# One broadcast matmul in place of two: the cached-key scores of a decoder trunk

## The chip, the cores and the metric

The kernel runs on 1 core of one Trainium2 chip. The metric is device time in microseconds (us) of one launch, taken as the median of several runs. Five engines work beside each other and meet at semaphores: TensorE (PE, matmuls), VectorE (DVE), ScalarE (ACT), GpSimd (POOL) and SyncE (SP), which issues most of the DMAs here; POOL issues the rest. Each engine works strictly in its own order.

## The reference

A two-layer decoder trunk in fp32 for 512 prompt tokens and 32 sample tokens (8 sequences of 4), width 1024. Layer 0 mixes by pooling; layer 1 is dilated attention with three head groups. Cut to the part that the change touches, the keys and values are projected once, and the sample queries see 128 cached keys of each group beside the new ones:

```python
kv_new = (x @ attn_w_kv).reshape(b, n, N_DIL_GROUPS, 2, HEADS_PER_GROUP, HEAD_DIM)
for g in range(N_DIL_GROUPS):
    kv_g = jnp.concatenate([kv_past[g], kv_new[:, :, g]], axis=1)
    kv_groups.append((kv_g[:, :, 0], kv_g[:, :, 1]))
...
idx = rows[:, None] - steps[None, :]
kg = jnp.take(k, idx, axis=1, mode='clip')
s = jnp.einsum('bqhd,bqkhd->bhqk', q_blk, kg)
```

In group 0 (dilation 1) all four queries of a sequence look at the same cached keys. In groups 1 and 2 (dilation 4 and 16) each of the four looks at keys of its own.

## The kernel before, in words

**Products.** Every linear layer is computed from split operands: a value is a high part (rounded to fp32r) and a low part (what is left). `products` (L602) runs, for each of 8 chunks k of 128 input features, three pairs of matmuls (high weight by high input, high by low, low by high), each pair covering the 544 tokens as 2 x 272 columns. Such a step is called an eighth here, and `products` of one 128-wide output chunk a unit. Weights arrive by DMA in `raw[s]`, s = 0 or 1; ACT writes the high part (`round_hi`, L1060), DVE the low part (`round_lo`, L1342), and SP may load `raw[s]` anew once the low part is made (`stream`, L464).

**The key/value stage** has 12 turns i, each of two units, s = 0 and s = 1. On PE (`kv_turn`, L833) a turn is: unit 0 of turn i, the transposes of chunk s = 1 of turn i-1, unit 1, the transposes of chunk s = 0. `kv_transposes` (L789) turns a feature-major chunk `kvt[s]` to token-major: four 128 x 128 transposes for the prompt (L794) and one piece for the 32 samples (L796). That piece is an ordinary fp32 matmul by the identity, which writes 32 partitions of a bank of `pc`, partitions 0 to 31 for s = 0 and 32 to 63 for s = 1. A transpose is told to the hardware as such by `nc.tensor.transpose`; the plain `matmul` at L796 is not. ACT evacuates both (`kv_tokens`, L1241), and SP stores them.

**Scores on cached keys** ride in turns 2 to 9, one sequence b in each (b = 0 to 7). Group 0: PE turns the sequence's 128 keys (`turn_keys`, L802), DVE copies them (L1564), PE multiplies (`key_scores`, L810). Groups 1 and 2: for each of 8 steps t (2 groups x 4 queries) the query's row must stand on all 128 partitions beside the keys. `cast_queries` (L820) does that on PE. The stationary operand is a one-hot tile `sel[s]` of 32 rows x 128 columns that picks one of 32 query rows, and the moving operand is the 32 query rows, 512 columns. Since the rows are split in a high and a low part (`q_hi`, `q_lo`, 32 rows each), it takes two matmuls of 512 columns into one bank (L829). Then DVE multiplies with the keys (L1544, `times`) and sums (L1552, `summed`). Steps 1 to 4 ride in unit 0, one in front of every second eighth, and steps 5 to 8 in unit 1. The order written out for DVE (`kv_turn`, L1555) puts the two weight roundings of a turn between those: the low part for s = 1 behind `times` of step 2, and for s = 0 of the next turn behind `times` of step 6:

```python
                if t == 2:
                    round_lo("kv", 1, i)
                if t == 6:
                    round_lo(nxt, 0, j)
                summed(b, t)
```

PE may overwrite the bank for step t + 1 only when `times` of step t is done (`kq_made`, L827). On ACT (`kv_turn`, L1251) a turn is: evacuate unit 0, `round_hi` for s = 0 of the next turn, tokens of s = 1, evacuate unit 1, `round_hi` for s = 1, tokens of s = 0. On SP (L535) the weights of turn i + 1 for s = 0 stand behind the store of the tokens of s = 0 of turn i - 1.

**Loading keys.** POOL, when sequence b is done, writes the one-hot tile and the group-0 queries for sequence b + 2 (`queries`, L1769) and then issues its keys' load, three DMAs of 2.25 MB together (`load`, L1757). For sequences 0 and 1 this stands ahead of the stage, so the loads for sequences 2 to 7 are issued at the start of turns 3 to 8 of the stage.

Of the kernel before, what the change touches and what calls it, by code (L numbers as in the profile page):

```python
# [42 lines left out]
GW = HEADS * DH  # L43
# [113 lines left out]
def build(nc, A, O):  # L157
# [3 lines left out]
    def sb(where, name, shape, dt=F32):  # L161
        return where.enter_context(nc.sbuf_tensor("t_" + name, shape, dt))

    def sem(name):
        return ctx.enter_context(nc.semaphore(name))

    with ctx:
# [8 lines left out]
        ident = sb(ctx, "ident", [P, P])  # L176
# [4 lines left out]


        rq = ExitStack()
        q_hi = sb(rq, "q_rows_hi", [SAMP, 2 * GW], F32R)
        sel = [sb(rq, "one_hot0", [SAMP, DEC_S, P], F32R)]
        rq.close()
        elem = sb(ctx, "elementwise", [P, 3 * T])
        sg, hf, sq = (elem[:, j * T:(j + 1) * T] for j in range(3))
        tab = sb(ctx, "bias_rows", [HEADS, NG, RP])
        s_bias = sb(ctx, "samp_bias", [P, NG * (P + BW)])  # L190
        s_sc = sb(rq, "samp_scores", [P, NG, 256])
        q_lo = sb(rq, "q_rows_lo", [SAMP, 2 * GW], F32R)
        sel += [sb(rq, "one_hot1", [SAMP, DEC_S, P], F32R)]
        rq.close()
        work = sb(ctx, "work", [P, 5 * T])
        accs, accq, mean, var, rstd = (work[:, j * T:(j + 1) * T] for j in range(5))
# [48 lines left out]
        kvt = [sb(hq, f"kv_feat{s}", [P, T]) for s in range(2)]  # L245
# [27 lines left out]
        kv_n = sb(rx, "kv_new", [SAMP, NG * 2 * GW])  # L273
# [15 lines left out]
        pa, pb, pc, pd = ps  # L289
# [60 lines left out]
        kv_t = [sem(f"kv_transposed{s}") for s in range(2)]  # L350
        kv_tok = [sem(f"kv_tok_ready{s}") for s in range(2)]
# [22 lines left out]
        kc_ok = sem("cached_keys_evacuated")  # L374
        kc_used = sem("cached_keys_used")
        qrow_t = sem("q_rows_turned")
        qhi_ok = sem("q_rows_hi")
        qlo_ok = sem("q_rows_lo")
        q_cast = sem("q_on_all_partitions")
# [221 lines left out]
        def _(pe):  # L601
# [131 lines left out]
            for g, out in enumerate((pa[:, 0, :], pa[:, 1, :], pb[:, 0, :])):  # L733
                m = nc.tensor.matmul(out[0:HEADS, 0:RP], rbx[:, g * HEADS:(g + 1) * HEADS], oh_t[:, g, :],
                                     start=True, stop=True)
            m.then_inc(tab_mm, 1)
            for v in range(6):
                for half, cols in enumerate((slice(0, NG * P), slice(NG * P, NG * (P + BW)))):
                    m = nc.tensor.matmul(pc[:, half, 0:cols.stop - cols.start], rb_s[:, v, :], oh_s[:, v, cols],
                                         start=v == 0, stop=v == 5)  # L740
# [12 lines left out]
            for c in range(DC):  # L753
                m = nc.tensor.transpose(pc[0:PAD + SAMP, c // 4, (c % 4) * P:(c % 4 + 1) * P], utail[:, c, :], ident[:])
            m.then_inc(utail_t, 1)

            for g in range(4):
                for s in range(2):
# [5 lines left out]
                    m = products(ps[s], s, 2, lambda k: phi[:, 2 * g + k, :], lambda k: plo[:, 2 * g + k, :], at=2 * g)  # L764
# [24 lines left out]
            def kv_transposes(s, i, first=False):  # L789
                pe.wait_ge(kv_evac[s], i + 1)  # L790
                if not first:
                    pe.wait_ge(kv_tok[s], 2 * i)
                for j in range(QB):
                    nc.tensor.transpose(ps[2 + s][:, 0, j * P:(j + 1) * P], kvt[s][:, j * P:(j + 1) * P], ident[:])  # L794

                nc.tensor.matmul(pc[SAMP * s:SAMP * (s + 1), 1, 0:P], kvt[s][:, SEQ:T], ident[:], start=True,  # L796
                                 stop=True).then_inc(kv_t[s], 1)

# [19 lines left out]
            def cast_queries(b, s, t):  # L820

                g, i = (t - 1) // 4, (t - 1) % 4
                if t == 1:
                    pe.wait_ge(qb_ok, b + 1)
                    pe.wait_ge(kc_ok, b + 1)
                else:
                    pe.wait_ge(kq_made, (NCK - 1) * b + t - 1)  # L827
                for n, part in enumerate((q_hi, q_lo)):
                    m = nc.tensor.matmul(pd[:, 1, :], sel[s][:, i, :], part[:, g * GW:(g + 1) * GW], start=n == 0,  # L829
                                         stop=n == 1)  # L830
                m.then_inc(q_cast, 1)

            def kv_turn(i, b=None, s=0):  # L833

# [19 lines left out]
            for g in range(2):  # L854
                for c in range(GC):
                    m = nc.tensor.transpose(pc[0:SAMP, g, c * P:(c + 1) * P], qt[:, (g + 1) * GC + c, SEQ:T], ident[:])
# [2 lines left out]
            kv_units(0, 0, True)  # L859
            kv_units(1, 0, True)  # L860
            pe.wait_ge(qlo_ok, 1)
            kv_transposes(0, 0, True)
            kv_units(0, 1)
            kv_transposes(1, 0, True)
# [40 lines left out]
            for g in range(NG):  # L905
                for c in range(GC):
                    row = pb[0:SAMP, g // 2, (g % 2) * 256:(g % 2 + 1) * 256]
                    m = nc.tensor.matmul(row.rearrange("p (b c n) -> p b c n", b=DEC_B, c=GC)[:, :, c, :],
                                         kn_t[:, g * GC + c, :],
                                         q_bd[:, g * GC + c, :].rearrange("p (b n) -> p b n", b=DEC_B),  # L910
                                         start=True, stop=True)
# [33 lines left out]
            for c in range(GC):  # L945
                for g in range(NG):
# [3 lines left out]
                                         start=g == 0, stop=g == NG - 1)  # L950
# [106 lines left out]
        def _(act):  # L1057
# [127 lines left out]
            for c in range(DC):  # L1185
                s = c % 2
# [54 lines left out]
            def kv_tokens(s, i, first=False):  # L1241
                act.wait_ge(kv_t[s], i + 1)
                if not first:
                    act.wait_ge(kv_out[s], 32 * i)
                nc.scalar.activation(kvp[s][:].rearrange("p j n -> p (j n)"), ps[2 + s][:, 0, :], ACT.Copy) \
                    .then_inc(kv_tok[s], 1)
                nc.scalar.activation(kv_n[:, bass.ds((2 * i + s) * P, P)], pc[SAMP * s:SAMP * (s + 1), 1, 0:P],
                                     ACT.Copy) \
                    .then_inc(kv_tok[s], 1)

            def kv_turn(i, stored, nxt, j, keys=None, b=None):  # L1251
# [4 lines left out]
                kv_tokens(0, i)  # L1256

            act.wait_ge(qrow_t, 1)
            nc.scalar.activation(q_hi[:], pc[0:SAMP].rearrange("p a n -> p (a n)"), ACT.Copy).then_inc(qhi_ok, 1)
            kv_chunk(0, 0, 0, "kv", 1, True, keys=0)  # L1260
            kv_chunk(1, 0, 0, "kv", 1, True, keys=0)
            kv_tokens(0, 0, True)
# [76 lines left out]
        def _(dve):  # L1339
# [190 lines left out]
            def q_turn(i, nxt, j):  # L1530
# [4 lines left out]


            dve.wait_ge(qhi_ok, 1)
            nc.vector.tensor_tensor(q_lo[:], pc[0:SAMP].rearrange("p a n -> p (a n)"), q_hi[:].bitcast(F32), ALU.subtract) \
                .then_inc(qlo_ok, 1)

            def times(b, s, t):

# [168 lines left out]
        def _(pool):  # L1711
# [51 lines left out]
            def load_keys(b, s):  # L1763
                load(b, cached[s][:, 0, :], cached[s][:, 1:NCK, :], 0, cached_in[s])
# [2 lines left out]
                load(b, v_c0[s][:], v_c[s], 1, value_in[s])  # L1767

            def queries(b, s):  # L1769
                nc.gpsimd.tensor_copy(sel[s][:], ident[0:SAMP, bass.ds(DEC_S * b, DEC_S)].unsqueeze(2)  # L1770
                                      .to_broadcast([SAMP, DEC_S, P]))
                nc.gpsimd.tensor_copy(q_b[s][:], q_bd[:, 0:GC, bass.ds(2 * DEC_S * b, 2 * DEC_S)]).then_inc(qb_ok, 1)

            for s in range(2):
                pool.wait_ge(w_used[s], FIRST["kv"])
            load_keys(0, 0)
            load_keys(1, 1)
            nc.gpsimd.memset(q_bd[:], 0.0).then_inc(qbd_ok, 1)
            pool.wait_ge(qbd_ok, 1)
            pool.wait_ge(q_evac, NG * GC)  # L1780
# [71 lines left out]
```

## Time and profile before

| | us |
|---|---|
| median of 3 runs | 2517.81 |
| lowest, highest run | 2512.13, 2519.68 |
| span of the profiled execution | 2516.9 |
| PE busy in it | 2315.5 (92%) |
| DVE, ACT, POOL busy | 920.3, 680.1, 262.3 |
| DMA over the span | 99 GB/s |

The profiled execution has no time of its own beside its span; the span is 0.9 us under the median and within the runs' spread, so it is taken for its time. In the rows below, `128*32` behind an operation is rows by columns of the part of the PE array that it uses, and `128x512` partitions by elements. The start of a record is when the engine took it up; matmuls are pipelined, so the distance from one start to the next, and not the duration, is what one costs in a stream. The printed code carries the line numbers of the profile.

### The profile page before, as it was taken

Reading aid. Unit: us, or ns where it says so; the run is one execution under the profiler, and the core shown is the slowest. Engines: PE = TensorE matmul, PEld = TensorE weight load, DVE = VectorE, ACT = ScalarE, POOL = GpSimd, SP = SyncE. Lnnn points to the kernel's source line nnn. Section 1 sums busy time; section 2 is a strip of 40 time slices with the busy share of each in tenths; the row PEclk is TensorE's granted clock in tenths of the full one; section 3 lists DMA queues with packets and bytes.
Section 4 is the critical chain, followed back from the end, with each engine's and each line's share of the span. In section 5 each row is a group of like instructions: output and inputs, shape, how many; then the busy total and the mean of one; then the engine's idle time right before and its main releaser. Section 6 shows DMA issues by size and latency. Waiting matters only on the chain.

```text
span 2516.9 us, 42260 instructions
## 1 busy us (share of the span) xinstructions
PE 2315.5 (92%) x17471; PEld 2168.3 (86%) x17471; DVE 920.3 (37%) x1176; ACT 680.1 (27%) x956; POOL 262.3 (10%) x241
## 2 busy tenths in 40 slices
PE   7559999978799999979999989999988988999997
PEld 5559999978799999979999979877854468999996
DVE  2113332276633332243333233366433344333324
ACT  3112222233422222232222223222222234222212
POOL 0000001211300001210000230111011040000022
PEclk9779999989899999989999999999979998999998
DMA  3542233212222233232323342565464222232331
GB/s 98 80 92 83 87 97 92 75 59 62 62 87 85 84 100 90 77 127 87 88 87 93 91 134 71 180 196 180 146 213 140 90 67 59 83 92 83 98 92 47
DMA packets 376249, 248.81 MB, mean 99 GB/s; under 512 B 7807, under 2 KB 360423, under 8 KB 375631
## 3 DMA queue, kind: packets, MB, share of 16 engines
q1 hardware_dynamic: 366087, 209.95, 29.3%
q0 software_dynamic: 10096, 37.94, 4.3%
q8 instruction: 47, 0.77, 0.1%
q14 instruction: 19, 0.15, 0.0%
HBM read 225.91 MB, written 22.31 MB: 99 GB/s over the span
## 4 chain that ended last, share of the span: by engine, by line
PE 85%; DMA 6%; DVE 5%; ACT 2%; issue 1%; SPq 1%; POOL 1%; DVEq 0%; POOLq 0%; ACTq 0%
PE pair L610 71%; DMA t_w_raw<-in_ffn_w 4%; PE pair L630 3%; PE pair L962 3%; PE pair L829 2%; DVE t_stream L1434 1%; PE pair L709 1%; PE pair L887 1%; DMA t_w_raw<-in_attn_w_kv 1%; DVE t_work L1436 1%; PE pair L985 1%; PE pair L995 1%; ACT t_w_hi L1068 1%; DVE t_w_lo L1348 1%; DMA t_bias<-scratch_bias_rows 1%
## 5 line engine op out<-in xcount | busy, mean ns | idle before, releaser
L1348 DVE TENSOR_TENSOR t_w_lo<-t_w_raw,t_w_hi 128x1024 fp32r<-128x1024 f32 (+2 forms) x302 | 421.3, 1395 | 834.8 <-ACT t_w_hi L1068 834.7
L610 PE MATMUL pair<-t_x_hi,t_w_hi 128*128 128x272 f32 x2944 | 618.5, 292 | 66.0 <-DVE t_w_lo L1348 63.5
L610 PE MATMUL pair<-t_x_lo,t_w_hi 128*128 128x272 f32 x2944 | 613.1, 289 | 0.0
L610 PE MATMUL pair<-t_x_hi,t_w_lo 128*128 128x272 f32 x2944 | 612.6, 289 | 0.0
L1068 ACT ACTIVATE t_w_hi<-t_w_raw 128x1024 fp32r<-128x1024 f32 (+2 forms) x302 | 336.3, 1114 | 947.1 <-PE pair L610 842.4
L610 PEld LDWEIGHTS pair<-t_x_hi,t_w_hi 128*128 128x128 f32 x2944 | 466.1, 190 | 67.9 <-DVE t_w_lo L1348 57.3
L610 PEld LDWEIGHTS pair<-t_x_lo,t_w_hi 128*128 128x128 f32 x2944 | 470.6, 191 | 0.0
L610 PEld LDWEIGHTS pair<-t_x_hi,t_w_lo 128*128 128x128 f32 x2944 | 465.5, 190 | 0.0
L610 PE MATMUL pair<-t_h_hi,t_w_hi 128*128 128x272 f32 x1408 | 292.2, 289 | 0.0
L610 PE MATMUL pair<-t_h_lo,t_w_hi 128*128 128x272 f32 x1408 | 290.3, 287 | 0.0
L610 PE MATMUL pair<-t_h_hi,t_w_lo 128*128 128x272 f32 x1408 | 290.0, 287 | 0.0
L1723 POOL TENSOR_TENSOR t_work<-t_work,t_stream 128x544 f32<-128x544 f32 x42 | 59.1, 1408 | 1613.9 <-DVE t_stream L1410 1612.4
L610 PEld LDWEIGHTS pair<-t_h_lo,t_w_hi 128*128 128x128 f32 x1408 | 222.1, 188 | 0.0
L610 PEld LDWEIGHTS pair<-t_h_hi,t_w_hi 128*128 128x128 f32 x1408 | 219.7, 188 | 0.0
L610 PEld LDWEIGHTS pair<-t_h_hi,t_w_lo 128*128 128x128 f32 x1408 | 219.7, 188 | 0.0
L1107 ACT ACTIVATE t_elementwise<-pair 128x544 f32<-128x544 f32 x88 | 55.0, 625 | 387.5 <-PE pair L610 387.5
L1399 DVE TENSOR_TENSOR t_elementwise<-t_elementwise,pair 128x544 f32<-128x544 f32 x88 | 63.4, 721 | 261.7 <-PE pair L610 260.9
L1410 DVE SCALAR_TENSOR_TENSOR t_stream<-pair,t_stream 128x544 f32 (+1 forms) x48 | 34.8, 725 | 218.0 <-PE pair L610 218.0
L630 PE MATMUL pair<-t_x_hi,t_w_hi 128*128 128x272 f32 x192 | 45.0, 319 | 63.1 <-DVE t_x_lo L1449 63.1
L1725 POOL TENSOR_TENSOR t_work<-t_work,t_elementwise 128x544 f32<-128x544 f32 x42 | 102.7, 2444 | 0.0
L630 PEld LDWEIGHTS pair<-t_x_hi,t_w_hi 128*128 128x128 f32 x192 | 34.4, 215 | 65.3 <-issue 65.3
L610 PE MATMUL pair<-t_kv_in_hi,t_w_hi 128*128 128x272 f32 x384 | 89.2, 313 | 0.0
(222 smaller groups left out, 2223.9 us busy)
## 6 DMA issues: line engine op xcount, KB each, us to landing
t_w_raw<-in_ffn_w SPq DMA_DIRECT2D x176, 512.0 KB, 3.8
t_w_raw<-in_ffn_w SPq DMA_DIRECT2D x64, 704.0 KB, 4.5
t_cached<-in_cache_kv_w POOLq DMA_DIRECT2D x16, 1024.0 KB, 9.3
t_cached_v<-in_cache_kv_w POOLq DMA_DIRECT2D x16, 1024.0 KB, 8.1
t_w_raw<-in_attn_w_kv SPq DMA_DIRECT2D x24, 512.0 KB, 6.9
t_w_raw<-in_attn_w_q SPq DMA_DIRECT2D x12, 512.0 KB, 3.7
scratch_bias_rows<-t_bias_rows SPq DMA_DIRECT2D x3, 1536.0 KB
t_w_raw<-in_pool_w_in SPq DMA_DIRECT2D x8, 512.0 KB, 3.6
```

The lines of the kernel that those rows point to most:

```text
L610: m = nc.tensor.matmul(out[:, j, 0:HALF], w[:, at + k, :], a(k)[:, j * HALF:(j + 1) * HALF], start=first and k == 0 and n == 0, stop=last ...
L630: m = nc.tensor.matmul(ps[s][:, j, 0:HALF], w[:, k, :], a[:, k, j * HALF:(j + 1) * HALF], start=k == 0 and n == 0, stop=k == DC - 1 and n ...
L709: m = nc.tensor.matmul(out[:, j, 0:HALF], invd[:], a[:, j * HALF:(j + 1) * HALF], start=first, stop=not first)
L829: m = nc.tensor.matmul(pd[:, 1, :], sel[s][:, i, :], part[:, g * GW:(g + 1) * GW], start=n == 0, stop=n == 1)
L962: m = nc.tensor.matmul(pd[32 * s:32 * s + 32, 0, :], p_b[s][:, t, :], v_c0[s][:] if t == 0 else v_c[s][:, t - 1, :], start=t == 0, stop=t ...
L1068: nc.scalar.activation(whi[s][:, 0:KT[stage], :], raw[s][:, 0:KT[stage], :], ACT.Copy) \
L1107: nc.scalar.activation(split(sg[:]), halves(pa), ACT.Silu).then_inc(gate_silu, 1)
L1348: nc.vector.tensor_tensor(wlo[s][:, 0:k, :], raw[s][:, 0:k, :], whi[s][:, 0:k, :].bitcast(F32), ALU.subtract).then_inc(lo_made[s], 1)
L1399: nc.vector.tensor_tensor(split(hf[:]), split(sg[:]), halves(pb), ALU.mult).then_inc(h_made, 1)
L1410: nc.vector.scalar_tensor_tensor(out=split(x[:, c, :]), in0=halves(out), scalar=scale, in1=split(x[:, c, :]), op0=ALU.mult, op1=ALU.add) \
L1723: nc.gpsimd.tensor_tensor(accs[:], accs[:], x[:, c, :], ALU.add).then_inc(acc_made, 1)
L1725: nc.gpsimd.tensor_tensor(accq[:], accq[:], sq[:], ALU.add).then_inc(acc_made, 1)
```

## The change

The high and low query rows are stacked in one tile `q_hl` of 128 partitions: rows 0 to 31 high, 32 to 63 low, 64 to 127 zero. The one-hot tiles become 128 x 4 x 128, with the one-hot twice (rows 0 to 31 and 32 to 63) and zero below, so that one matmul over all 128 rows adds high and low part. The one-hots are now cut from `id2`, the 32 x 32 identity twice. POOL builds `id2` and the zeros once, ahead of its q-block work, and PE waits for that (`qsel_ok`) before its first transposes of the stage. The samples' piece of `kv_transposes` becomes a real transpose, always to partitions 0 to 31, with s = 0 in columns 0 to 127 and s = 1 in columns 128 to 255 of the same bank; PE now also waits, ahead of the transposes of one s, until ACT has evacuated the tokens of the other s before it.

```diff
-        q_hi = sb(rq, "q_rows_hi", [SAMP, 2 * GW], F32R)
-        sel = [sb(rq, "one_hot0", [SAMP, DEC_S, P], F32R)]
+        q_hl = sb(rq, "q_rows", [P, 2 * GW], F32R)
+        sel = [sb(rq, "one_hot0", [P, DEC_S, P], F32R)]
...
-        q_lo = sb(rq, "q_rows_lo", [SAMP, 2 * GW], F32R)
-        sel += [sb(rq, "one_hot1", [SAMP, DEC_S, P], F32R)]
+        sel += [sb(rq, "one_hot1", [P, DEC_S, P], F32R)]
+        id2 = sb(rq, "ident_twice", [2 * SAMP, SAMP])
...
                 if not first:
                     pe.wait_ge(kv_tok[s], 2 * i)
+                if not (first and s == 0):
+                    pe.wait_ge(kv_tok[1 - s], 2 * (i + s))
...
-                nc.tensor.matmul(pc[SAMP * s:SAMP * (s + 1), 1, 0:P], kvt[s][:, SEQ:T], ident[:], start=True,
-                                 stop=True).then_inc(kv_t[s], 1)
+                nc.tensor.transpose(pc[0:SAMP, 1, s * P:(s + 1) * P], kvt[s][:, SEQ:T], ident[:]).then_inc(kv_t[s], 1)
...
-                for n, part in enumerate((q_hi, q_lo)):
-                    m = nc.tensor.matmul(pd[:, 1, :], sel[s][:, i, :], part[:, g * GW:(g + 1) * GW], start=n == 0,
-                                         stop=n == 1)
-                m.then_inc(q_cast, 1)
+                nc.tensor.matmul(pd[:, 1, :], sel[s][:, i, :], q_hl[:, g * GW:(g + 1) * GW], start=True, stop=True) \
+                    .then_inc(q_cast, 1)
...
             pe.wait_ge(qlo_ok, 1)
+            pe.wait_ge(qsel_ok, 3)
             kv_transposes(0, 0, True)
...
-                nc.gpsimd.tensor_copy(sel[s][:], ident[0:SAMP, bass.ds(DEC_S * b, DEC_S)].unsqueeze(2)
-                                      .to_broadcast([SAMP, DEC_S, P]))
+                nc.gpsimd.tensor_copy(sel[s][0:2 * SAMP], id2[:, bass.ds(DEC_S * b, DEC_S)].unsqueeze(2)
+                                      .to_broadcast([2 * SAMP, DEC_S, P]))
...
+            for h in range(2):
+                part = slice(SAMP * h, SAMP * h + SAMP)
+                nc.gpsimd.tensor_copy(id2[part], ident[part, part]).then_inc(qsel_ok, 1)
+            nc.gpsimd.memset(q_hl[2 * SAMP:P, :].bitcast(F32), 0.0)
+            for s in range(2):
+                m = nc.gpsimd.memset(sel[s][2 * SAMP:P].bitcast(F32), 0.0)
+            m.then_inc(qsel_ok, 1)
+            pool.wait_ge(qsel_ok, 3)
```

The ACT copy of the high rows, the DVE subtraction for the low rows and the ACT evacuation of the samples' piece only change the places that they read and write.

PE, the first broadcast of turn 2 and the group-0 scores behind it, before:

```order
L610 MATMUL pair<-t_kv_in_hi,t_w_lo 128x272 x2
L829 MATMUL pair<-t_q_rows_hi,t_one_hot 128x512 [waits cached_keys_evacuated,q_blocks_b_ready]
L829 MATMUL pair<-t_q_rows_lo,t_one_hot 128x512
L610 MATMUL pair<-t_kv_in_hi,t_w_hi 128x272 x2
L610 MATMUL pair<-t_kv_in_lo,t_w_hi 128x272 x2
L610 MATMUL pair<-t_kv_in_hi,t_w_lo 128x272 x2
L815 MATMUL pair<-t_q_blocks_b,t_k_turned 128x8 [waits cached_keys_evacuated,q_blocks_b_ready]
```

The same place now (lines of the changed kernel stand one or two lower):

```order
L611 MATMUL pair<-t_kv_in_hi,t_w_lo 128x272 x2
L830 MATMUL pair<-t_q_rows,t_one_hot 128x512 [waits cached_keys_evacuated,q_blocks_b_ready]
L611 MATMUL pair<-t_kv_in_hi,t_w_hi 128x272 x2
L611 MATMUL pair<-t_kv_in_lo,t_w_hi 128x272 x2
L611 MATMUL pair<-t_kv_in_hi,t_w_lo 128x272 x2
L817 MATMUL pair<-t_q_blocks_b,t_k_turned 128x8 [waits cached_keys_evacuated,q_blocks_b_ready]
```

One matmul is gone at each of the 64 places like this one, and nothing else moved between them.

POOL, behind the issue of the first keys and ahead of the first one-hots, as a piece of the difference:

```order
 L1761 DMA t_cached<-in_cache_kv_w 128x4x512
-L1778 MEMSET t_q_blocks 128x768
-L1783 COPY t_q_blocks<-t_q_feat 64x384 [waits q_evac,q_blocks_ready]
-L1783 COPY t_q_blocks<-t_q_feat 64x384
-L1770 CAST t_one_hot<-t_ident 32x512 [waits q_blocks_ready]
+L1780 COPY t_ident_twice<-t_ident 32x32 x2
+L1781 MEMSET t_q_rows 64x1024
+L1783 MEMSET t_one_hot 64x512 x2
+L1786 MEMSET t_q_blocks 128x768 [waits one_hots_zeroed]
+L1791 COPY t_q_blocks<-t_q_feat 64x384 [waits q_evac,q_blocks_ready]
+L1791 COPY t_q_blocks<-t_q_feat 64x384
+L1770 CAST t_one_hot<-t_ident_twice 64x512 [waits q_blocks_ready]
```

Five small operations come in front of the q-block work, and the one-hot copies cover 64 partitions in place of 32.

## Rows read from the trace of the kernel before

**Rows 1.** The page: busy time by engine, and the chain that ended last, by line.

```profile
PE 2315.5 (92%) x17471; PEld 2168.3 (86%) x17471; DVE 920.3 (37%) x1176; ACT 680.1 (27%) x956; POOL 262.3 (10%) x241
...
PE pair L610 71%; DMA t_w_raw<-in_ffn_w 4%; PE pair L630 3%; PE pair L962 3%; PE pair L829 2%; DVE t_stream L1434 1%; PE pair L709 1%; PE pair L887 1%; DMA t_w_raw<-in_attn_w_kv 1%; DVE t_work L1436 1%; PE pair L985 1%; PE pair L995 1%; ACT t_w_hi L1068 1%; DVE t_w_lo L1348 1%; DMA t_bias<-scratch_bias_rows 1%
```

**Rows 2.** Windows: start:end, us; busy (x count) by engine; PEclk, DMA share, GB/s.

```profile
1660.00:1680.00 20.00, 19.87 (x125) 15.48 (x124) 11.46 (x18) 4.83 (x10) 2.81 (x5) 1.00 0.64 208
```

**Rows 3.** Timeline of PE, a broadcast and the eighths around it: start us, us, what.

```profile
1647.74 0.42 PE L610 MATMUL pair<-t_kv_in_hi,t_w_lo 128*128 128x272 f32 x2
1648.08 0.50 PE L829 MATMUL pair<-t_q_rows_hi,t_one_hot 32*128 32x512 f32 x1
1648.42 0.39 PE L829 MATMUL pair<-t_q_rows_lo,t_one_hot 32*128 32x512 f32 x1
1648.74 0.52 PE L610 MATMUL pair<-t_kv_in_hi,t_w_hi 128*128 128x272 f32 x2
1649.09 0.41 PE L610 MATMUL pair<-t_kv_in_lo,t_w_hi 128*128 128x272 f32 x2
...
1650.10 0.42 PE L610 MATMUL pair<-t_kv_in_hi,t_w_lo 128*128 128x272 f32 x2
1650.44 0.50 PE L829 MATMUL pair<-t_q_rows_hi,t_one_hot 32*128 32x512 f32 x1
```

**Rows 4.** Timeline of PE: start of one turn and of the next.

```profile
1662.36 0.60 PE L794 MATMUL pair<-t_ident,t_kv_feat 128*128 128x128 f32 x4
1662.89 0.41 PE L796 MATMUL pair<-t_ident,t_kv_feat 128*32 128x128 f32 x2
1663.22 0.66 PE L807 MATMUL pair<-t_ident,t_cached 128*128 128x128 f32 x4
...
1684.66 0.60 PE L794 MATMUL pair<-t_ident,t_kv_feat 128*128 128x128 f32 x4
```

**Rows 5.** Timeline of PE: turning the sample queries ahead of the stage.

```profile
1590.07 1.05 PE L856 MATMUL pair<-t_ident,t_q_feat 128*32 128x128 f32 x8 [0.71 <-ACT t_q_feat L1224]
1590.88 0.50 PE L610 MATMUL pair<-t_kv_in_hi,t_w_hi 128*128 128x272 f32 x2
```

**Rows 6.** Timeline of ACT in the turn that starts at 1662.36.

```profile
1674.92 0.62 ACT L1238 ACTIVATE t_kv_feat<-pair 128x544 f32<-128x544 f32 x1
1676.71 1.06 ACT L1068 ACTIVATE t_w_hi<-t_w_raw 128x1024 fp32r<-128x1024 f32 x1 [1.17 <-DMA t_w_raw<-in_attn_w_kv]
```

**Rows 7.** Timeline of the SP queue in that turn.

```profile
1665.73 0.93 SPq L468 DMA_DIRECT2D t_w_raw<-in_attn_w_kv  x1
```

**Rows 8.** Waits, 1625 to 1830 us: total us, times, longest us.

```profile
ACT t_w_hi L1068 <- DMA t_w_raw<-in_attn_w_kv: 5.9, 6, 1.6
```

**Rows 9.** Windows of 2 us in that turn, as in rows 2.

```profile
1670.00:1672.00 2.00, 2.00 (x14) 1.47 (x12) 1.85 (x4) 0.00 (x0) 0.00 (x0) 1.00 0.98 376
```

**Rows 10.** Timeline of DVE in that turn.

```profile
1679.18 0.69 DVE L1544 TENSOR_TENSOR t_k_times_q<-pair,t_cached 128x512 f32<-128x512 f32 x1 [0.85 <-PE pair L829]
1679.79 1.22 DVE L1348 TENSOR_TENSOR t_w_lo<-t_w_raw,t_w_hi 128x1024 fp32r<-128x1024 f32 x1
...
1681.55 0.69 DVE L1544 TENSOR_TENSOR t_k_times_q<-pair,t_cached 128x512 f32<-128x512 f32 x1
```

**Rows 11.** Timeline of POOL ahead of the first turn.

```profile
1594.07 0.79 POOL L1778 MEMSET t_q_blocks<- 128x768 f32 x1
...
1596.11 0.60 POOL L1770 CAST t_one_hot<-t_ident 32x512 fp32r<-32x512 f32 x1
```

**Rows 12.** Timeline of PE: the first turn with broadcasts starts.

```profile
1618.64 0.66 PE L807 MATMUL pair<-t_ident,t_cached 128*128 128x128 f32 x4 [0.67 <-DVE t_w_lo L1348]
```

**Rows 13.** Timeline of ACT behind the stage.

```profile
1829.99 0.60 ACT L1245 ACTIVATE t_kv_tok<-pair 128x512 f32<-128x512 f32 x1 [4.16 <-DMA out_kv_p<-t_kv_tok]
```

**Rows 14.** Windows of the attention behind the stage, as in rows 2.

```profile
1880.00:1900.00 20.00, 17.89 (x138) 9.29 (x138) 6.33 (x19) 3.79 (x7) 5.29 (x16) 1.00 0.58 172
1900.00:1920.00 20.00, 19.15 (x120) 9.00 (x123) 8.04 (x26) 5.65 (x13) 0.00 (x0) 0.83 0.33 112
```

More of the change, by code:

```diff
@@ L376, in build @@
         qrow_t = sem("q_rows_turned")
+        qsel_ok = sem("one_hots_zeroed")
         qhi_ok = sem("q_rows_hi")
@@ L1246, in kv_tokens @@
                     .then_inc(kv_tok[s], 1)
-                nc.scalar.activation(kv_n[:, bass.ds((2 * i + s) * P, P)], pc[SAMP * s:SAMP * (s + 1), 1, 0:P],
-                                     ACT.Copy) \
+                nc.scalar.activation(kv_n[:, bass.ds((2 * i + s) * P, P)], pc[0:SAMP, 1, s * P:(s + 1) * P], ACT.Copy) \
                     .then_inc(kv_tok[s], 1)
@@ L1258, in _ @@
             act.wait_ge(qrow_t, 1)
-            nc.scalar.activation(q_hi[:], pc[0:SAMP].rearrange("p a n -> p (a n)"), ACT.Copy).then_inc(qhi_ok, 1)
+            nc.scalar.activation(q_hl[0:SAMP, :], pc[0:SAMP].rearrange("p a n -> p (a n)"), ACT.Copy).then_inc(qhi_ok, 1)
             kv_chunk(0, 0, 0, "kv", 1, True, keys=0)
@@ L1537, in _ @@
             dve.wait_ge(qhi_ok, 1)
-            nc.vector.tensor_tensor(q_lo[:], pc[0:SAMP].rearrange("p a n -> p (a n)"), q_hi[:].bitcast(F32), ALU.subtract) \
-                .then_inc(qlo_ok, 1)
+            nc.vector.tensor_tensor(q_hl[SAMP:2 * SAMP, :], pc[0:SAMP].rearrange("p a n -> p (a n)"),
+                                    q_hl[0:SAMP, :].bitcast(F32), ALU.subtract).then_inc(qlo_ok, 1)
             def times(b, s, t):
```

## The prediction

> **What bounds the kernel now.** I read the page first. PE is busy 92% of the span, and the chain that ended last lies on PE for most of its length; the broadcasts, L829, are 2% of it, some 50 us [rows 1]. Then the windows of the key/value stage, because the change lives there alone. From 1660 to 1680 us PE is busy 19.87 of 20 us at the full granted clock, the DMA engines 0.64 and DVE 11.46 of 20 us [rows 2]. So in this stage PE is the bound, and time taken off PE comes off the end, until another engine is late. Then the timeline of a turn on PE for the prices, and last ACT, SP and DVE in the same turn, to see who is late next.
>
> **What a broadcast costs.** From one broadcast to the next is 1648.08 to 1650.44, 2.36 us. In it lie two eighths, six pairs of matmuls. Four pairs take 1649.09 to 1650.10, 1.01 us, so a pair takes 0.2525 us and six take 1.515 us. The broadcast costs the rest, **0.845 us**, although its two matmuls start only 0.34 us apart [rows 3]. The remainder sits at the edges: 0.34 us from the last pair to the broadcast, and 0.35 us for the first pair behind it, where 0.25 is usual. The new one has all 128 rows and the same fp32r type as its neighbours. Its matmul is the kind of L610: 272 columns start 0.126 us apart, of which 0.113 are the columns at 2.4 GHz, so 512 columns take 0.213 + 0.013 = 0.227 us; I take 0.24. The upper bound: only one of the two starts goes and the edges stay, 0.845 - 0.34 = 0.505 us. Between them I take the low end, since the row it is nearest to is a full-array fp32r matmul in a stream. The saving is 0.6 us a broadcast (0.34 to 0.62), 4.8 us in a turn of eight.
>
> The Trainium skill (TensorE: Matmul & The Clock Gate, Part 3, The mechanism) has a rule against this: a weight load overlaps a running matmul only if its row group differs. Its Part 2 (LDWEIGHTS) prices a load at columns over 1.2 GHz, an estimate of 107 ns for 128. With full-array operands every broadcast would carry that load in the open, 0.33 us, and the sum would be 2 us smaller (16 broadcasts and the six last ones below, 0.09 each). The trace disagrees: L610 changes 128-column weights before every matmul and still starts one each 0.126 us [rows 3].
>
> **The samples' transposes.** Today the four prompt transposes and the sample piece take 0.53 + 0.33 = 0.86 us [rows 4]. L856, eight real transposes of the 128*32 shape that the new ones have, takes 0.81 us, 0.10 each [rows 5]. At that pace the four are 0.41, so 0.12 of the 0.53 is an edge ahead of the other kind of matmul. The new group is 0.41 + 0.10, plus 0.05 for what edge is left: 0.56 us, **0.3 us** less (bounds: 0, if a lone one costs what L796 does, and 0.34).
>
> The Trainium skill (TensorEngine Tiling (Array Packing), Restrictions) excludes the transpose mode for fp32 when columns are tiled. By it the piece would stay as dear as it is and some 2.7 us of the sum would go. Eight such f32 pieces at 0.10 us speak against it [rows 5].
>
> **A turn if PE alone decides.** A turn lasts 1662.36 to 1684.66, 22.30 us [rows 4]. It loses 4.8 and 2 x 0.3: 16.9 us.
>
> **Who is late next.** In the turn from 1662.36 ACT evacuates unit 0 at 1674.92 and then waits 1.17 us for the weights of s = 0; it starts rounding at 1676.71, 14.35 us after the turn began [rows 6]. Six turns have that wait, 0.98 us on average [rows 8], so the mean is 14.2. They are the six in which POOL loads keys. SP issued these weights at 1665.73, 3.4 us into the turn [rows 7], tied to the tokens of the turn before and not to the broadcasts, and they share the DMA engines with 2.25 MB of keys, which run at 0.98 busy and 376 GB/s [rows 9]. Nothing here gets faster by the change: the weights still land 14.2 us into the turn. Behind that stands a chain that is covered now: rounding on ACT 1.06 us; the low part on DVE, then `summed` of step 6 and `times` of step 7, which ends 1681.55 + 0.69 - 1679.79 = 2.45 us after the low part starts [rows 6, 10]; the broadcast of step 8, which PE may not start before `times` of step 7 is done, 0.05 + 0.24; the last eighth, 0.76. In sum 14.2 + 1.06 + 2.45 + 0.29 + 0.76 = **18.8 us**. PE alone wants 16.9, so PE stands idle about 1.9 us ahead of the last broadcast of these turns. They shrink by 22.3 - 18.8 = 3.5 us, six times: **21 us**. The cost of a broadcast no longer matters much in them.
>
> The other two turns with broadcasts (b = 0, whose keys came early, and b = 7, behind which no keys are loaded) have no such wait and go to 16.9: 2 x 5.4 = **10.8 us**. DVE holds there, though barely: from `times` of step 6 to the end of `times` of step 7, with the rounding between, is 1681.55 + 0.69 - 1679.18 = 3.06 us [rows 10], and PE takes two eighths and one broadcast, 1.75 + 1.5 = 3.27 us, over the same steps.
>
> The transposes outside those eight turns: the first turns end in front of L807, where PE waits 0.67 us for a weight rounding [rows 12], so nothing is won there; five groups behind the last broadcast give 5 x 0.3 = **1.5 us**.
>
> **What it adds.** POOL: three memsets of 1024, 512 and 512 elements and two small copies. A memset of 768 takes 0.79 us [rows 11], so they take 2.1 us, the copies at most 0.4. POOL's first one-hot then comes at 1598.6 in place of 1596.1, and the first broadcast is behind 1618.64 [rows 12]: nothing. PE's wait on the zeros stands behind both units of turn 0, 16 eighths from 1590.88 [rows 5], at 1603, later too. If that cover were gone it would cost the 2.5 us once. The larger one-hot copy: 32 x 512 took 0.60 us [rows 11], and cost goes by elements in a partition, so I price 64 x 512 the same; 0.6 us more in front of each key load would be the upper bound, 3.6 us. The new waits on the other s: in a turn ACT has the tokens of s = 0 done before SP's issue at 3.4 us, long before PE needs them; those of s = 1 follow the late rounding, two copies behind 15.3, at about 16 us of 18.8. In the first turns they fall where PE waits already [rows 12]. At the very end PE stands until ACT has made the last tokens of s = 0, two copies or some 0.9 us, and ACT behind it waits 4.16 us for a store anyway [rows 13]. All of it: 0.
>
> **The sum.** 21 + 10.8 + 1.5 = 33.3 us. The profiled execution had a span of 2516.9, 0.9 under the median, so from the median 2517.8 - 33.3 = **2484.5**. What follows the stage starts from the end of its last units and moves with it.
>
> **The rivals.**
> (a) The weights are not late: with PE ahead of DVE's rounding the queue meets less traffic, or they land 2 us earlier. Then all eight turns go to 16.9, 8 x 5.4 + 1.5 = 44.7: 2473. Against it: the wait stands in six of six turns with keys. Chance 0.15.
> (b) They land later, by 1 to 3 us: the other weights and the stores are issued sooner in the shorter turn and compete with the keys, and DVE has only 0.2 us of margin. Each us costs 6 us; or a broadcast stays at its upper bound, turns 19.0: 26.4 + 1.5 gives 2490. Together 2490 to 2502. Chance 0.21.
> (c) The change hardly pays: the weights land 3.5 us later in the six turns, which takes their 21 us back, and DVE's margin turns out negative in the other two. That leaves 0 to 7 us, 2510 to 2518. For it the weights would have to take 14.5 us from issue to landing in place of 11, with the same bytes beside them. Chance 0.04.
> (d) Slower: the clock. PE now stands idle 1.9 us in each of six turns. If the grant fell to 1.2 GHz from that, each such turn would pay its 16 eighths again, 16 x 0.76 = 12.1 us; three turns of six eat the whole gain, six give 2484.5 + 73 = 2557. For it: in the attention a window with PE busy 19.15 of 20 us shows 0.83. Against it: one with 17.89 shows 1.00 [rows 14], and a turn would still be 90% busy with full-array products. Chance 0.06.
> The Trainium skill (TensorE: Matmul & The Clock Gate, Part 4) says that transpose mode does not count as busy for the clock, which would add to (d) with 24 more transposes. Turns with eight of them and more run at 1.00 [rows 2].
>
> **How the numbers follow.** The forecast, 2479 to 2490, has 0.54, (a) 0.15, (b) 0.21, (c) 0.04, (d) 0.06. The range takes in (a) with 2 us for the spread of runs, and (b) up to 2502: 2471 to 2502. What a measurement can tell from no change is about 0.3%, 7.5 us. Faster by more: 0.54 + 0.15 + 0.21 = 0.90. Within: 0.04. Slower: 0.06.
>
> **What would show it.** Right: broadcasts followed by a pair after 0.24 us; sample transposes 0.10 us; turns of 18.8 us where keys are loaded and 16.9 where not; DVE's low part for s = 0 waiting about 2 us for ACT, ACT for the weights about 3 us, and PE for `times` ahead of the last broadcast; DMA share about 0.75 over a turn. Wrong: even turns of 16.9 us (a); ACT's wait above 4 us (b); a granted clock under 1.00 between 1620 and 1790 us (d).

## The result, and the profile after

| | before | after |
|---|---|---|
| median, us | 2517.57 (4 runs) | 2487.08 (4 runs) |
| span of the profiled execution, us | 2516.9 | 2486.0 |
| PE busy, us | 2315.5 | 2271.2 |

The medians are 30.5 us apart. The ratio of the times, estimated from the single runs, is 0.9874, with a 95% interval of 0.9861 to 0.9888; the quotient of the medians, 0.9879, lies in it. So the changed kernel is faster, by 1.1 to 1.4%. (The kernel before was run once more beside it, so its median is of four runs now.) The page of the kernel after, its first lines and its chain, to be read against [rows 1]:

```profile
PE 2271.2 (91%) x17383; PEld 2157.6 (87%) x17383; DVE 917.7 (37%) x1176; ACT 679.4 (27%) x956; POOL 265.9 (11%) x246
...
PE pair L611 68%; DMA t_w_raw<-in_ffn_w 4%; PE pair L631 3%; PE pair L963 3%; DMA t_w_raw<-in_attn_w_kv 3%; DVE t_stream L1434 1%; PE pair L710 1%; PE pair L888 1%; DVE t_work L1436 1%; PE pair L986 1%; ACT t_w_hi L1069 1%; PE pair L996 1%; DVE t_u_sum L1476 1%; DMA t_bias<-scratch_bias_rows 1%; DVE t_w_lo L1348 0%
```

The broadcasts, 2% of the chain before, no longer stand among its parts; the load of the key/value weights has 3% in place of 1%. That is the story in one line: time went off PE, and a DMA came forward. PE is busy for 44 us less, and only 31 us of that reach the end. (Lines of the changed kernel stand one to three lower on PE and ACT: L611 for L610, L797 for L794, L799 for L796, L809 for L807, L830 for L829, L1069 for L1068.)

The timeline of PE after, one broadcast and the next, answers [rows 3]:

```profile
1659.64 0.42 PE L611 MATMUL pair<-t_kv_in_hi,t_w_lo 128*128 128x272 f32 x2
1659.89 0.40 PE L830 MATMUL pair<-t_q_rows,t_one_hot 128*128 128x512 f32 x1
1660.13 0.41 PE L611 MATMUL pair<-t_kv_in_hi,t_w_hi 128*128 128x272 f32 x2
...
1661.39 0.42 PE L611 MATMUL pair<-t_kv_in_hi,t_w_lo 128*128 128x272 f32 x2
1661.65 0.50 PE L830 MATMUL pair<-t_q_rows,t_one_hot 128*128 128x512 f32 x1
```

From broadcast to broadcast is 1.76 us, less six pairs of 0.2525 leaves **0.245 us** for the broadcast, where it was 0.845. The pair ahead and the pair behind are at their usual distance: 1659.64 to 1659.89, 1660.13 to 1660.38 (not shown). The edges are gone. The group of transposes in the middle of the turn, which answers [rows 4]:

```profile
1662.75 0.60 PE L797 MATMUL pair<-t_ident,t_kv_feat 128*128 128x128 f32 x4
1663.19 0.27 PE L799 MATMUL pair<-t_ident,t_kv_feat 128*32 128x128 f32 x1
1663.21 0.50 PE L611 MATMUL pair<-t_kv_in_hi,t_w_hi 128*128 128x272 f32 x2
1663.56 0.41 PE L611 MATMUL pair<-t_kv_in_lo,t_w_hi 128*128 128x272 f32 x2
```

It takes 0.46 us from its first transpose to the next product, 0.09 us for each of five. The same group in the middle of a turn took 0.87 us before. The group at the start of a turn, up to the turning of the keys (L807, now L809), went from 0.86 to 0.54 us.

The starts of turns on PE, same view. The first two rows enclose a turn with a key load (b = 5), the last two the one without (b = 7):

```profile
1711.04 0.60 PE L797 MATMUL pair<-t_ident,t_kv_feat 128*128 128x128 f32 x4
...
1729.63 0.60 PE L797 MATMUL pair<-t_ident,t_kv_feat 128*128 128x128 f32 x4
...
1747.53 0.60 PE L797 MATMUL pair<-t_ident,t_kv_feat 128*128 128x128 f32 x4
...
1764.51 0.60 PE L797 MATMUL pair<-t_ident,t_kv_feat 128*128 128x128 f32 x4
```

The eight turns last 17.1, 19.1, 20.5, 19.2, 18.0, 18.6, 17.9 and 17.0 us. The six in the middle load keys; their mean is 18.9. All eight were 22.3.

Why the six are longer is in the turn from 1653.40, in which three engines hand one delay on. ACT first, waiting for the weights:

```profile
1668.33 1.06 ACT L1069 ACTIVATE t_w_hi<-t_w_raw 128x1024 fp32r<-128x1024 f32 x1 [4.28 <-DMA t_w_raw<-in_attn_w_kv]
```

then DVE, in the order written for it:

```profile
1666.22 0.69 DVE L1544 TENSOR_TENSOR t_k_times_q<-pair,t_cached 128x512 f32<-128x512 f32 x1 [0.21 <-PE pair L830]
1669.43 1.23 DVE L1348 TENSOR_TENSOR t_w_lo<-t_w_raw,t_w_hi 128x1024 fp32r<-128x1024 f32 x1 [2.52 <-ACT t_w_hi L1069]
1670.57 0.68 DVE L1552 TENSOR_REDUCE t_samp_scores<-t_k_times_q 128x512 f32 x1
1671.16 0.68 DVE L1544 TENSOR_TENSOR t_k_times_q<-pair,t_cached 128x512 f32<-128x512 f32 x1
```

then PE, whose last broadcast of the turn needs the product at 1671.16:

```profile
1669.03 0.42 PE L611 MATMUL pair<-t_kv_in_hi,t_w_lo 128*128 128x272 f32 x2
1671.90 0.79 PE L830 MATMUL pair<-t_q_rows,t_one_hot 128*128 128x512 f32 x1 [2.46 <-DVE t_k_times_q L1544]
```

The weights land 14.9 us into this turn, the latest of the six (13.2 to 14.9, 14.1 on average; before, 13.3 to 14.6, also 14.1 on average). PE stands 2.46 us, the longest of six such gaps; the others are 0.8 to 1.93 us, and the mean is 1.5. Over the stage, the waits view of 1625 to 1790 us after, against [rows 8]:

```profile
ACT t_w_hi L1069 <- DMA t_w_raw<-in_attn_w_kv: 21.4, 7, 4.3
PE pair L830 <- DVE t_k_times_q L1544: 9.0, 6, 2.5
```

ACT's wait for weights went from 5.9 to 21.4 us, of which 20.5 us are the six turns with key loads: the weights land when they did, counted from the start of a turn, and the rest of the turn reaches them sooner.

### The profile page after: what moved, and what is told of

It is laid out like the page before. It is cut to its first block, busy times and chain, and to the rows that moved or that the text cites. A ratio compares the mean times of both kernels' runs of the same rounds, so it can differ in the third digit from the quotient of the medians.

```text
span 2486.0 us, 42096 instructions
## 1 busy us (share of the span) xinstructions
PE 2271.2 (91%) x17383; PEld 2157.6 (87%) x17383; DVE 917.7 (37%) x1176; ACT 679.4 (27%) x956; POOL 265.9 (11%) x246
## 4 chain that ended last, share of the span: by engine, by line
PE 81%; DMA 8%; DVE 5%; ACT 2%; issue 2%; SPq 1%; POOL 1%; ACTq 0%; DVEq 0%; POOLq 0%
PE pair L611 68%; DMA t_w_raw<-in_ffn_w 4%; PE pair L631 3%; PE pair L963 3%; DMA t_w_raw<-in_attn_w_kv 3%; DVE t_stream L1434 1%; PE pair L710 1%; PE pair L888 1%; DVE t_work L1436 1%; PE pair L986 1%; ACT t_w_hi L1069 1%; PE pair L996 1%; DVE t_u_sum L1476 1%; DMA t_bias<-scratch_bias_rows 1%; DVE t_w_lo L1348 0%
## 5 line engine op out<-in xcount | busy, mean ns | idle before, releaser
L611 PE MATMUL pair<-t_x_hi,t_w_hi 128*128 128x272 f32 x2944 | 616.7, 291 | 67.1 <-DVE t_w_lo L1348 64.6
L611 PE MATMUL pair<-t_x_lo,t_w_hi 128*128 128x272 f32 x2944 | 611.6, 289 | 0.0
L611 PE MATMUL pair<-t_x_hi,t_w_lo 128*128 128x272 f32 x2944 | 610.8, 289 | 0.0
L1069 ACT ACTIVATE t_w_hi<-t_w_raw 128x1024 fp32r<-128x1024 f32 (+2 forms) x302 | 336.8, 1115 | 964.3 <-PE pair L611 839.4
L611 PEld LDWEIGHTS pair<-t_x_hi,t_w_hi 128*128 128x128 f32 x2944 | 464.1, 190 | 69.0 <-DVE t_w_lo L1348 58.3
L611 PEld LDWEIGHTS pair<-t_x_lo,t_w_hi 128*128 128x128 f32 x2944 | 469.0, 190 | 0.0
L611 PEld LDWEIGHTS pair<-t_x_hi,t_w_lo 128*128 128x128 f32 x2944 | 463.9, 189 | 0.0
L611 PE MATMUL pair<-t_h_hi,t_w_hi 128*128 128x272 f32 x1408 | 292.2, 289 | 0.0
L611 PE MATMUL pair<-t_h_lo,t_w_hi 128*128 128x272 f32 x1408 | 290.3, 287 | 0.0
L611 PE MATMUL pair<-t_h_hi,t_w_lo 128*128 128x272 f32 x1408 | 290.0, 287 | 0.0
L611 PEld LDWEIGHTS pair<-t_h_lo,t_w_hi 128*128 128x128 f32 x1408 | 222.1, 188 | 0.0
L611 PEld LDWEIGHTS pair<-t_h_hi,t_w_hi 128*128 128x128 f32 x1408 | 219.7, 188 | 0.0
L611 PEld LDWEIGHTS pair<-t_h_hi,t_w_lo 128*128 128x128 f32 x1408 | 219.7, 188 | 0.0
L611 PE MATMUL pair<-t_kv_in_hi,t_w_hi 128*128 128x272 f32 x384 | 82.3, 296 | 0.0
```

Source lines behind the costliest of these rows:

```text
L611: m = nc.tensor.matmul(out[:, j, 0:HALF], w[:, at + k, :], a(k)[:, j * HALF:(j + 1) * HALF], start=first and k == 0 and n == 0, stop=last ...
L1069: nc.scalar.activation(whi[s][:, 0:KT[stage], :], raw[s][:, 0:KT[stage], :], ACT.Copy) \
```

## The experiments

Each kernel was run beside the kernel before on the same chip, whose medians there were 2516.84 us (the first four) and 2516.27 us (the last four). Theory: a broadcast's price is mostly the change of array shape, and with it gone the late weights, passed on by DVE, set the six turns. The rivals: the second matmul itself is the price; DVE's order alone sets the six turns, whatever the weights do; every microsecond of PE still counts.

**The two halves of the change apart.** The broadcast alone, with the samples' piece and the waits as before:

```diff
-                if not (first and s == 0):
-                    pe.wait_ge(kv_tok[1 - s], 2 * (i + s))
...
-                nc.tensor.transpose(pc[0:SAMP, 1, s * P:(s + 1) * P], kvt[s][:, SEQ:T], ident[:]).then_inc(kv_t[s], 1)
+                nc.tensor.matmul(pc[SAMP * s:SAMP * (s + 1), 1, 0:P], kvt[s][:, SEQ:T], ident[:], start=True,
+                                 stop=True).then_inc(kv_t[s], 1)
```

> The one-matmul broadcast alone: the samples' piece and PE's waits are those of the kernel before. Theory (in the six turns with key loads the end is set by the late weights for s = 0, through DVE, and only the turns of b = 0 and b = 7 are PE's): those two turns are 0.6 us longer than in the changed kernel (17.7 in place of 17.1 and 17.0), the six with key loads as long (mean 18.9), so the whole takes 2488 to 2489.5 us, 28 us or more under the kernel before. Rival (PE's time counts in every turn): 8 x 0.6 us, 2492 us.

Measured: 2486.86 us, ratio 0.9877 (0.9862 to 0.9893). The first turn is 17.8 us long and the six with key loads 18.75 on average, 18.3 to 19.1. So without the transposes the gain is there as far as the medians (2486.9 and 2487.1) can tell. The turns came out as expected; the total is 1 to 3 us under it. The turns at either end are 0.8 us longer than in the changed kernel, 1.6 us in all, and the medians don't show that; in the profile of the changed kernel one turn lost about as much to the clock (below), and here none did. The rival's 2492 is outside.

The transposes and the new waits alone, in the kernel before (the reverse of this diff):

> The real transposes of the samples' piece and the new waits on the other s alone; the broadcasts stay two matmuls of 32 rows. Here PE sets every turn, so both see a gain of two pieces a turn: turns of 22.3 - 2 x 0.32 = 21.7 us, eight of them 5 us, in all 2511 to 2513 us. If the new waits cost something where PE is the bound, less than that: PE would stand idle ahead of L794, which the waits view would name. Behind the stage I expect no gain, since ACT waits there for a store.

Measured: 2510.25 us, ratio 0.9974 (0.9966 to 0.9983), 6.6 us less than before. The starts of two neighbouring turns:

```profile
1680.96 0.60 PE L808 MATMUL pair<-t_ident,t_cached 128*128 128x128 f32 x4
...
1702.45 0.60 PE L808 MATMUL pair<-t_ident,t_cached 128*128 128x128 f32 x4
```

Turns of 21.5 us, 0.8 less than 22.3, so a piece saves 0.40 us and not 0.3: eight turns give 6.4 us. The same edit is worth 6.6 us where PE is the bound, and nothing in the six turns that late weights set (18.75 us without it, 18.9 with it). PE stops at the new waits twice, 1.1 us ahead of the first turn with broadcasts and 0.9 us at the very end. From the turning of the sample queries to the first turned keys it still takes 27.9 us, where it took 28.6 before, and at the end ACT waits for a store anyway, so this kernel shows no cost of them.

**What a broadcast costs.** Both matmuls kept, but padded with zeros to all rows, in the kernel before:

```diff
-        q_hi = sb(rq, "q_rows_hi", [SAMP, 2 * GW], F32R)
-        sel = [sb(rq, "one_hot0", [SAMP, DEC_S, P], F32R)]
+        q_hi = sb(rq, "q_rows_hi", [P, 2 * GW], F32R)
+        sel = [sb(rq, "one_hot0", [P, DEC_S, P], F32R)]
...
+            for rest in (slice(SAMP, 2 * SAMP), slice(2 * SAMP, P)):
+                nc.gpsimd.memset(q_hi[rest, :].bitcast(F32), 0.0)
+                nc.gpsimd.memset(q_lo[rest, :].bitcast(F32), 0.0)
+                for s in range(2):
+                    m = nc.gpsimd.memset(sel[s][rest].bitcast(F32), 0.0)
```

> The kernel before with both broadcast matmuls kept, but each over all 128 rows: one-hot, high rows and low rows are padded with zeros. Theory (most of the 0.845 us of a broadcast is at the edges, where the array changes from 128 rows to 32 and back): a broadcast costs 0.45 to 0.47 us, both matmuls start 0.23 us apart, and the first pair behind takes 0.25 us; a turn is 22.3 - 3.0 = 19.3 us, eight of them save 24 us, about 2494 us. Rival (the two matmuls cost what they do because they are two): 0.85 us stays, 2517 us.

Measured: 2493.97 us, ratio 0.9907 (0.9892 to 0.9923). PE's timeline:

```profile
1645.73 0.40 PE L830 MATMUL pair<-t_q_rows_hi,t_one_hot 128*128 128x512 f32 x1
1645.96 0.39 PE L830 MATMUL pair<-t_q_rows_lo,t_one_hot 128*128 128x512 f32 x1
1646.19 0.41 PE L611 MATMUL pair<-t_kv_in_hi,t_w_hi 128*128 128x272 f32 x2
1646.44 0.41 PE L611 MATMUL pair<-t_kv_in_lo,t_w_hi 128*128 128x272 f32 x2
```

Two matmuls in 0.46 us and no edge behind them; turns of 19.3 to 19.4 us, one of 19.9. With the same columns to stream and the same number of matmuls as before, 22.9 of the 30 us are there. So most of the gain is not the matmul saved but the rows padded. The 22.9 overstate its share, because the late weights cap what is saved further in six turns; by the price of a broadcast it is 0.38 of the 0.60 us saved.

The changed kernel with its one matmul over the 64 rows that are not zero:

```diff
-                nc.tensor.matmul(pd[:, 1, :], sel[s][:, i, :], q_hl[:, g * GW:(g + 1) * GW], start=True, stop=True) \
+                nc.tensor.matmul(pd[:, 1, :], sel[s][0:2 * SAMP, i, :], q_hl[0:2 * SAMP, g * GW:(g + 1) * GW],
+                                 start=True, stop=True) \
```

> The changed kernel, but the one broadcast matmul reads only the 64 rows that are not zero. Theory of the edges: the array changes to 64 rows and back, so a broadcast costs 0.23 + 0.1 + 0.1 + 0.1 = about 0.5 us in place of 0.24; turns of b = 0 and 7 grow by 2 us to 19.1, the six others to about 19.2 at least, in all 2491 to 2494 us. Rival (one matmul in place of two is the whole gain, the zero rows do nothing): 0.24 us, 2487 us.

Measured: 2497.04 us, ratio 0.9916 (0.9899 to 0.9933). PE's timeline:

```profile
1647.84 0.41 PE L611 MATMUL pair<-t_kv_in_hi,t_w_lo 128*128 128x272 f32 x2
1648.18 0.50 PE L830 MATMUL pair<-t_q_rows,t_one_hot 64*128 64x512 f32 x1
1648.61 0.52 PE L611 MATMUL pair<-t_kv_in_hi,t_w_hi 128*128 128x272 f32 x2
1648.97 0.42 PE L611 MATMUL pair<-t_kv_in_lo,t_w_hi 128*128 128x272 f32 x2
...
1650.33 0.50 PE L830 MATMUL pair<-t_q_rows,t_one_hot 64*128 64x512 f32 x1
```

One matmul over 64 rows costs 2.15 - 1.515 = 0.635 us, more than two over 128 rows (0.465). It has 0.09 us more than usual ahead, 0.43 from its start to the next pair where the full one has 0.24, and 0.11 more behind: 0.39 us of edges. I had put them at 0.3 or less, hence turns of 19.65 us in place of 19.1 and a total 3 us above what was expected. PE sets all eight turns here, so all are alike. Two matmuls of 32 rows pay 0.845 - 0.465 = 0.38 us over two of 128 rows, one of 64 rows pays 0.39 over one of 128: the surcharge comes once for a stay on fewer rows and not once for each matmul, which is why it is put down to the change of shape.

**Who sets the six turns.** The changed kernel with one issue on SP moved:

```diff
-                stream("kv", i)
-                if i >= 1:
-                    kt_store(i - 1, 0)
-                    if i >= 2:
-                        kv_store(i - 2, 1)
-                    kt_store(i - 1, 1)
-                    kv_store(i - 1, 0)
+                weights(i, 1)
+                kt_store(i - 1, 0)
+                if i >= 2:
+                    kv_store(i - 2, 1)
+                if i + 1 < UNITS["kv"]:
+                    weights(i + 1, 0)
+                kt_store(i - 1, 1)
+                kv_store(i - 1, 0)
```

(`weights(i, s)` is one half of `stream`; the loop runs from i = 1, with `weights(0, 0)`, `weights(0, 1)` and `weights(1, 0)` ahead of it.)

> The changed kernel with one order of SP moved: the weights for s = 0 are issued as soon as DVE has freed their buffer, near the end of the turn before, ahead of the stores of s = 1 features and s = 0 tokens and so ahead of the key load. Theory (their landing, 14.2 to 15 us into a turn, sets the six turns with key loads): ACT's wait for weights in these turns is gone, all eight turns are 17.0 us, 6 x 1.9 = 11 us less than the changed kernel, 2476 us. Rival (DVE's own order, rounding between the products of steps 6 and 7, or the DMA traffic as a whole sets them): turns of 18 us or more stay, 2483 to 2488.

Measured: **2473.16 us**, ratio 0.983 (0.9817 to 0.9844), faster than both the kernel before and the changed one. Two turn starts, and the window of 1660 to 1680 us, which answers [rows 2]:

```profile
1681.85 0.60 PE L817 MATMUL pair<-t_ident,t_cached 128*128 128x128 f32 x4
...
1698.82 0.60 PE L817 MATMUL pair<-t_ident,t_cached 128*128 128x128 f32 x4
```

```profile
1660.00:1680.00 20.00, 19.89 (x151) 19.08 (x150) 16.27 (x23) 4.66 (x11) 2.82 (x5) 1.00 0.77 256
```

All turns are 17.0 us, 17.1 at most, and PE is busy 19.89 of 20 us again, with DVE at 16.27 and the DMA engines at 0.77. From the first turned keys to the end of the eighth turn that is 11.3 us less. From the transposes of the queries ahead of the stage to the first turned keys are 26.7 us in place of 27.9, which I had left out: there the weights of turn 2 waited behind stores as well, and ACT waited 5.0 us for them, 0.3 us here. With these 1.1 us it is 12.4. (The same stretch is 28.5 and 28.6 us in the last two kernels below, whose SP order is that of the changed kernel, so it varies by 0.8 us by itself.) The medians are 43.1 and 30.5 us under those of the kernel before, 12.6 apart; the two ratios, 0.983 and 0.9874, put them 11 us apart. So the move is worth 11 to 13 us. The bytes are the same: between 1634 and 1765 us the weights take 4.0 us from issue to landing (median), and 9.1 us in the changed kernel.

The same move in the kernel before:

> The same move of SP's order in the kernel before. There PE alone sets a turn (22.3 us) and the late weights are covered, so both theories say no change: 2517.5 us, within 2 us, although ACT's wait for weights goes from 5.9 us in six turns to 0. A gain of more than 5 us would mean that the late weights cost time already before.

Measured: 2513.94 us, ratio 0.9993 (0.9984 to 1.0002). Turns of 22.3 us as before, no wait of ACT for weights left in the six turns. The interval holds 1; it reaches from 4 us less to 0.5 us more. The stretch ahead of the first turned keys is 0.7 us shorter in its profile, and nothing else of the stage is. So the move that is worth 11 to 13 us on the changed kernel is worth next to nothing here.

The changed kernel without its later key loads:

```diff
-                    load_keys(2 * n + s, s)
...
-                pe.wait_ge(cached_in[s], 24 * (b - s) + 48)
+                pe.wait_ge(cached_in[s], 48)
```

> The changed kernel without the key loads for sequences 2 to 7: their scores are computed from the keys of sequences 0 and 1, which stay in place, and 13.5 MB less are read. Theory: with no keys beside them the weights land about 4 to 5 us after their issue, 8 us into a turn, ahead of ACT's need at 10; all eight turns are 17.0 us, 2476 us, as with the moved order. Rival (DVE's order sets the six turns): they stay at 18 us or more, 2484 to 2488.

Measured: 2473.66 us, ratio 0.9827 (0.9812 to 0.9842). Two turn starts:

```profile
1684.28 0.60 PE L809 MATMUL pair<-t_ident,t_cached 128*128 128x128 f32 x4
...
1701.26 0.60 PE L809 MATMUL pair<-t_ident,t_cached 128*128 128x128 f32 x4
```

Turns of 17.0 us, and again 4.0 us from the issue of the weights to their landing. The total is 2.3 us under the 2476 expected. Taking the keys' bytes away does the same as issuing the weights ahead of them. Both leave DVE's order and work as they are, so DVE's order alone is ruled out.

DVE's rounding moved from step 6 to step 8 (`if t == 6` becomes `if t == 8`):

> The changed kernel with DVE's rounding for s = 0 of the next turn moved from behind the product of step 6 to behind that of step 8. Theory: the late weights no longer hold back the last broadcast, but unit 0 of the next turn needs the rounding at 17.5 us into the turn and the weights arrive at 14.2 to 15, high part at 16, low part at 17.5 to 18.3: six turns of 18.0 to 18.3 us in place of 18.9, 2482 to 2484 us. If the weights' landing did not matter, the move would change nothing or cost, since the copy of the turned keys then stands behind the rounding: 2487 to 2490.

Measured: 2480.93 us, ratio 0.9857 (0.9842 to 0.9873), turns of 17.7 to 18.1 us, 17.9 on average, 1 us under the changed kernel's six and 0.1 to 0.4 under what was expected; the waits view, 1625 to 1790 us:

```profile
PE pair L809 <- DVE t_w_lo L1348: 5.6, 7, 1.0
```

The last broadcast is free now, and PE waits ahead of turning the next keys (L809), 0.8 us a turn. It does not wait there for late weights, as I had expected. The first line is PE behind the turn of b = 0, whose weights came early (ACT rounds them at 1627.97); the second is DVE in a turn with a key load:

```profile
1635.85 0.66 PE L809 MATMUL pair<-t_ident,t_cached 128*128 128x128 f32 x4 [0.69 <-DVE t_w_lo L1348]
...
1688.16 1.22 DVE L1348 TENSOR_TENSOR t_w_lo<-t_w_raw,t_w_hi 128x1024 fp32r<-128x1024 f32 x1
```

PE waits 0.69 us behind the early weights as well, and DVE makes the low part without a wait for ACT in all eight turns. So here DVE's order, with the rounding as the last thing but one, sets all eight turns, at 17.7 us and more; that they came close to the 18.0 to 18.3 us forecast from the landing is luck. What the run does show is that PE's wait at the last broadcast goes when the rounding leaves its place ahead of the product of step 7. Where the consumer of a late load stands in DVE's order is worth 1 us a turn; the load in time is worth 2.

## Why the prediction was right

2484.5 us was forecast and 2487.08 measured, within the likeliest case, and the mechanism was the one forecast. Step by step:

- **The broadcast**: 0.24 us forecast, 0.245 measured. The upper bound of 0.505 fell. That full-array operands make the weight load visible, as the Trainium skill's rule on row groups has it (TensorE: Matmul & The Clock Gate, Part 3, The mechanism), is not what this case shows: 0.245 us is 512 columns and 0.03.
- **The turn where PE decides**: 16.9 forecast, 17.1 and 17.0 measured. DVE's margin of 0.2 us held.
- **The turns with key loads**: 18.8 forecast, 18.9 measured on average, and by the mechanism forecast. It is shown by two runs, weights issued earlier and keys left out, and the way through DVE by the third, its order moved. The spread, 17.9 to 20.5, was not forecast: the weights landed 13.2 to 14.9 us into a turn, and once the clock fell, which is 0.25 us of the mean. Without it the mean is 18.6, so the fit to 0.1 us is in part luck. PE's gap was put at 1.9 us and is 1.5; ACT's wait of about 3 us was 2.6 to 4.3, in one turn past the 4 us named as the sign of (b).
- **The sum over the eight turns**: 31.8 forecast, 1796.09 - 1617.04 less 1764.51 - 1617.19 = 31.7 measured.
- **The transposes**: sized at 0.3 us a piece, from the group at the start of a turn. That group did go from 0.86 to 0.54 us, but the one in the middle from 0.87 to 0.46, and a turn lost 0.8 us where PE is the bound, 0.40 a piece. In the changed kernel this hardly matters, since six of eight turns don't feel it. The rule of the Trainium skill that column tiling rules the transpose mode out for fp32 (TensorEngine Tiling (Array Packing), Restrictions) would have left this at nothing; here a group with a 128*32 transpose in it takes 0.09 us for each of its five.
- **What it adds**: nothing, as forecast. POOL's first one-hot came at 1598.44 (forecast 1598.6), and the copy over 64 partitions takes 0.61 us where the one over 32 took 0.60.
- **The step that failed** is the 1.5 us behind the last broadcast. PE's five groups there did get shorter, but what follows waits for ACT, and ACT for a store that stands in SP's queue behind eight bias loads. I had seen that wait, 4.16 us [rows 13], used it as cover for the new wait of PE, and not subtracted the gain of the same groups from it. The wait grew from 4.16 to 5.86 us. After:

```profile
1798.24 0.60 ACT L1246 ACTIVATE t_kv_tok<-pair 128x512 f32<-128x512 f32 x1 [5.86 <-DMA out_kv_p<-t_kv_tok]
```

From the end of the eighth broadcast turn to this copy are 33.9 us before and 33.7 after. The remaining 687 us to the end are 0.9 us longer after, which no run here explains; over all ten profiles of this document they are 685.7 to 690.4 us.
- **The clock rival** came true in one turn, in small. The windows of the kernel after:

```profile
1670.00:1672.00 2.00, 0.10 (x1) 0.10 (x1) 1.86 (x4) 0.03 (x1) 0.00 (x0) 0.90 0.50 146
1672.00:1674.00 2.00, 2.00 (x8) 1.90 (x9) 1.80 (x3) 0.00 (x0) 0.40 (x1) 0.50 0.06 18
```

PE stood still for 2.46 us; near the end of that the granted clock fell to 0.50, the lower of the two levels, 1.2 GHz, and stayed there until about 1675 us. Pairs took 0.45 us, and broadcast, eighth and transposes about 1.5 us more than at 1.00. In the other five turns, with gaps of up to 1.93 us, the clock stayed at 1.00. It is one event in one profile: that the gap brought it about is not tested, nor whether the other executions have it.

## What to carry to other kernels

Before counting columns of a small matmul in a dense stream, subtract: the distance between two of them less the stream between gives the true price, and here nearly half of it (0.38 of 0.845 us) was the change of array shape on either side, which zero rows to the full height remove. Once the bound engine is relieved, the size of the gain is set by the first load or rounding that was only just covered; find it by its time into the period, and ask whether its issue hangs on something it doesn't need. Here moving one issue ahead of two stores was worth nothing that the runs can tell before the change, and 11 to 13 us after it.

## What the runs showed of the hardware

A 512-column fp32r matmul between 128-row products costs 0.245 us with 128 rows, 0.635 with 64 rows, and two with 32 rows 0.845; two with 128 rows cost 0.465. So a single change to fewer rows and back costs 0.38 to 0.39 us, more than a whole further matmul (0.22), and I had expected 0.3. The page TensorEngine Tiling (Array Packing) of the Trainium skill (Key Properties) says that a change of tiling mode drains the engine. The trace agrees in so far as the pair of changes costs 0.39 us; a drain as such it does not show.

Weights of 512 KB, issued behind three key loads of 2.25 MB together, took a median of 9.1 us from issue to landing; issued ahead of the keys, or with no keys loaded, 4.0 us.
